# A two-block layer kernel on one core: the first layer's weight slabs in another order, one warming matmul less, and two small steps moved in the lead

## What is computed

```
xn = rms_norm(h, norm_mix[l])
proj = xn @ w_in[l]                       # 1024 x 7464
q, k, v, qi, ki, wi, sc_u, sc_b, sc_c, rw_z, gate_pre = split(proj)
q, k, qi, ki = partial_rope(...)          # rotation by position
y_a = dsa_attention(q, k, v, qi, ki, wi)  # top-64 by an index score
y_b = short_conv_mixer(...)
y_c = rwkv7_time_mix(rw_z, ...)
h = h + (sum over branches of sigmoid(gates) * (branch @ w_branch)) @ w_out
h = h + conv_glu_ffn(rms_norm(h, norm_ffn[l]), ...)
```

## Time and profile before

| | |
|---|---|
| Median of 3 runs | 1647.84 us (1647.72 to 1647.96) |
| The profiled execution | 1648.03 us, its span 1646.2 us |
| PE busy | 1632.2 us (99%), 11188 matmuls |
| DVE busy | 1188.4 us (72%) |
| ACT busy | 971.1 us (59%) |
| POOL busy | 187.3 us (11%) |
| Mean granted clock of PE | 0.999 |

### The profile page before, as it was taken

How to read it: one execution, slowest core, us unless ns; L and a number is a source line. 1 busy time by engine, 2 the same in 40 slices (tenths; PEclk the granted TensorE clock), 3 DMA queues, 4 the chain that set the end, 5 groups by cost and what they waited for, 6 DMA issues and landing times.

```text
span 1646.2 us, 27390 instructions
## 1 busy us (share of the span) xinstructions
PE 1632.2 (99%) x11188; PEld 1417.6 (86%) x11188; DVE 1188.4 (72%) x1666; ACT 971.1 (59%) x1485; POOL 187.3 (11%) x193
## 2 busy tenths in 40 slices
PE   9999999999999999999999999999999999999998
PEld 6999999988888999999988878778788887788886
DVE  7987447699888975547898885767756657667655
ACT  7674525555567565345555574665774556657743
POOL 0764400000002945100000000000000000000000
PEclk9999999999999999999999999999999999999999
DMA  7443534455545425525465546345445563444452
GB/s 277 169 154 115 188 104 135 173 186 197 186 170 202 161 97 162 166 90 191 138 225 190 189 164 217 128 135 176 141 167 178 181 209 133 146 163 152 141 192 77
DMA packets 48892, 270.11 MB, mean 164 GB/s; under 512 B 13632, under 2 KB 14656, under 8 KB 17024
## 3 DMA queue, kind: packets, MB, share of 16 engines
q1 hardware_dynamic: 38448, 265.22, 46.3%
q10 hardware_dynamic: 9712, 2.62, 0.7%
q0 software_dynamic: 608, 0.53, 0.2%
HBM read 266.51 MB, written 1.84 MB: 163 GB/s over the span
## 4 chain that ended last, share of the span: by engine, by line
PE 87%; DVE 9%; ACT 2%; issue 1%; DMA 1%; SPq 0%; DVEq 0%; ACTq 0%
PE bank L1768 15%; PE bank L1769 15%; PE bank L1773 15%; PE bank L1660 7%; PE bank L1705 7%; PE bank L1706 6%; PE bank L1710 6%; DVE w_low L1037 4%; PE bank L1665 3%; PE bank L2830 2%; DVE arena L1222 1%; PE bank L2130 1%; PE bank L2818 1%; PE bank L2862 1%; PE bank L2180 1%
## 5 line engine op out<-in xcount | busy, mean ns | idle before, releaser
L1037 DVE TENSOR_TENSOR w_low<-slab,w_high 128x2048 fp32r<-128x2048 f32 x249 | 574.1, 2314 | 203.5 <-ACT w_high L609 196.6
L609 ACT ACTIVATE w_high<-slab 128x2048 fp32r<-128x2048 f32 x249 | 470.5, 1896 | 110.0 <-PE bank L1773 89.3
L1768 PE MATMUL bank<-w_high,act 128*128 128x512 f32 x1120 | 444.4, 397 | 2.4 <-DVE arena L1231 1.0
L1769 PE MATMUL bank<-w_high,act 128*128 128x512 f32 x1120 | 437.1, 390 | 0.0
L1773 PE MATMUL bank<-w_low,act 128*128 128x512 f32 x1120 | 309.7, 390 | 0.0
L1705 PE MATMUL bank<-act,w_high 128*128 128x256 f32 x1024 | 258.6, 290 | 0.0
L1768 PEld LDWEIGHTS bank<-w_high,act 128*128 128x128 f32 x1120 | 210.4, 188 | 50.0 <-issue 6.9
L1706 PE MATMUL bank<-act,w_high 128*128 128x256 f32 x1024 | 251.7, 283 | 0.0
L1773 PEld LDWEIGHTS bank<-w_low,act 128*128 128x128 f32 x1120 | 210.2, 188 | 44.6
L1769 PEld LDWEIGHTS bank<-w_high,act 128*128 128x128 f32 x1120 | 210.6, 188 | 41.0
L1705 PEld LDWEIGHTS bank<-act,w_high 128*128 128x128 f32 x1024 | 195.8, 191 | 7.9 <-issue 5.6
(11 more groups left out here) (264 smaller groups left out, 1845.1 us busy)
## 6 DMA issues: line engine op xcount, KB each, us to landing
slab<-stream_a SPq DMA_DIRECT2D x143, 1024.0 KB, 4.9
slab<-stream_b SPq DMA_DIRECT2D x104, 1024.0 KB, 4.9
arena<-x_t SPq DMA_DIRECT2D x4, 256.0 KB, 6.9
slab<-stream_a ACTq DMA_DIRECT2D x2, 512.0 KB, 6.3
residual<-x_tok SPq DMA_DIRECT2D x1, 1024.0 KB, 11.6
lora_weights<-lora SPq DMA_DIRECT2D x2, 512.0 KB, 6.0
lora_weights<-final_rows SPq DMA_DIRECT2D x2, 512.0 KB, 6.1
d_inverse<-arena ACTq DMA_DIRECT2D x2, 256.0 KB, 4.0
```

Of the source, the lines that this page charges most:

```text
L609: line.did(eng.activation(core.wh[u % PARTS][:, 0:SLAB_WIDTH[u]], core.slab[u % SLABS][:, 0:SLAB_WIDTH[u]], ACT.Copy), core.sem("slab_high"))
L1037: line.did(line.eng.tensor_tensor(core.wl[u % PARTS][:, 0:SLAB_WIDTH[u]], core.slab[u % SLABS][:, 0:SLAB_WIDTH[u]], core.wh[u % PARTS][:, ...
L1768: eng.matmul(out, core.xh[:, at, columns_], wh[:, k, :], start=first and k == 0, stop=False, skip_group_check=True)
L1769: eng.matmul(out, core.xl[:, at, columns_], wh[:, k, :], start=False, stop=False, skip_group_check=True)
```

## The change

The first layer gets a list of units of its own in which ki stands second: w 0, ki, w 1, q 0, ... The plan's rows (products, banks) are kept and only change places. Because ki's products are counted late (at its turn, inside q 0), the part buffer of ki in a0 is given free by the count before it, three products (`row[2]`), which is the end of w 1. The host packs the first layer's stream in the new order. The lookups by position (`rows[u - 1]`, `UA["ki", 0]`, `first + u < 2`) are replaced by lookups by name. ki now waits for all of x. In the lead, the table load stands behind the rounding and split of slab 1 (now ki), and the rotation tables are copied there. The warming matmuls are five. The norm's spread and the steps behind it are put behind w 1, which is now the third unit. The list `behind_mid` stays as it was.

```
+UNITS_A0 = [UNITS_A[0], UNITS_A[2], UNITS_A[1]] + UNITS_A[3:]
...
+PLAN_A0 = [PLAN_A[0], PLAN_A[2], PLAN_A[1]] + PLAN_A[3:]
-PLANS = {"a0": PLAN_A, "a1": PLAN_A, "b0": PLAN_B, "b1": PLAN_B}
+PLANS = {"a0": PLAN_A0, "a1": PLAN_A, "b0": PLAN_B, "b1": PLAN_B}
...
-    SLAB_ENDS += [START[stage_].get("products", 0) + row[3] for row in PLANS[stage_]]
+    SLAB_ENDS += [START[stage_].get("products", 0) + (row[2] if stage_ == "a0" and row[0] == "ki" else row[3]) for row in PLANS[stage_]]
...
-        return steps + [("scaled", 2), ("scaled", 3), ("root_table", 0), ("round", 1), ("split", 1)]
+        return steps + [("scaled", 2), ("scaled", 3), ("round", 1), ("split", 1), ("root_table", 0), ("angles", 2)]
...
-        put(("w", 0), ("square", 0), ("square", 1), ("norm", 0), ("angles", 2))
+        put(("w", 0), ("square", 0), ("square", 1), ("norm", 0))
     amid(("w", 1), *([] if first else [("norm", 0)]), ("tables", 0))
-    put(("ki" if first else "w", 0 if first else 1), ("norm_x", 0))
-    put(("ki", 0), ("params", 0), ("highs", 0), ("lows", 0))
+    put(("w", 1), ("norm_x", 0))
+    put(("w", 1) if first else ("ki", 0), ("params", 0), ("highs", 0), ("lows", 0))
...
-    return woven(UNITS_A, first, lead_steps(first), after, mid, early=[("br2", 0), ("br2", 1)],
+    return woven(UNITS_A0 if first else UNITS_A, first, lead_steps(first), after, mid, early=[("br2", 0), ("br2", 1)],
                  late=[("br2", 1)], behind_mid=[("q", 0), ("gc", 2)] + [("w", 0)] * (not first))
...
+def unit_at(rows, kind, i):
+
+    return [row[0:2] for row in rows].index((kind, i))
...
+def first_fills(rows, u):
+
+    return rows[unit_at(rows, rows[u][0], 0)][4]
...
         if i and not begins:
-            eng.wait_ge(sem("slab_split").sem, 2)
+            eng.wait_ge(sem("slab_split").sem, u + 1)
...
     def ki(u):
 
         n, b = IDX_DIM + IDX_HEADS, rows[u][4][0][0]
+        eng.wait_ge(*sem("x_ready").upto(4))
         eng.wait_ge(sem("slab_split").sem, first + u + 1)
...
-    for _ in range(6):
+    for _ in range(5):
         eng.matmul(core.bank[6][:], flat(core, IDLE_)[:, 0:P], flat(core, IDLE_, 2), start=True, stop=True, skip_group_check=True)
...
-        for u, (kind, i) in enumerate(UNITS_A):
+        for u, (kind, i) in enumerate((UNITS_A0, UNITS_A)[layer]):
```

More of the change, by code:

```diff
@@ L706, in scalar_a @@
 def scalar_a(core, eng, line, stage):
-    rows, sem, bank, vec, layer = PLAN_A, core.sem, core.bank, core.vec, int(stage[1])
+    rows, sem, bank, vec, layer = PLANS[stage], core.sem, core.bank, core.vec, int(stage[1])
     def act(out, in_, func, tally=None, **kw):
@@ L795, in unit @@
                 made(core, eng, rows, u, m)
-                act(half_of(core, QS_ if kind == "q" else WS_, m), bank[rows[u - 1][4][m][0]][:], ACT.Copy, sem("qk_raw"),
+                act(half_of(core, QS_ if kind == "q" else WS_, m), bank[first_fills(rows, u)[m][0]][:], ACT.Copy, sem("qk_raw"),
                     scale=token_scale(core, m))
@@ L834, in ki_turn @@
     def ki_turn(_):
-        u = UA["ki", 0]
+        u = unit_at(rows, "ki", 0)
         b = rows[u][4][0][0]
@@ L1123, in vector_a @@
 def vector_a(core, eng, line, stage):
-    rows, sem, bank, vec, did = PLAN_A, core.sem, core.bank, core.vec, line.did
+    rows, sem, bank, vec, did = PLANS[stage], core.sem, core.bank, core.vec, line.did
     layer = int(stage[1])
@@ L1244, in unit @@
             for m in range(2):
-                b = rows[u - 1][4][m][0]
+                b = first_fills(rows, u)[m][0]
                 by = lambda ap, d: ap.rearrange("p (h d) -> p h d", d=d)
@@ L1297, in ki_turn @@
     def ki_turn(_):
-        b, spare = rows[UA["ki", 0]][4][0][0], flat(core, AROPE_, 2)
+        b, spare = rows[unit_at(rows, "ki", 0)][4][0][0], flat(core, AROPE_, 2)
         eng.wait_ge(*sem("qk_raw").next(eng, 2))
@@ L1824, in tensor_a @@
 def tensor_a(core, eng, banks, stage):
-    rows, sem, bank, first = PLAN_A, core.sem, core.bank, FIRST_SLAB[stage]
+    rows, sem, bank, first = PLANS[stage], core.sem, core.bank, FIRST_SLAB[stage]
     mm = eng.matmul
@@ L1872, in begin @@
             return
-        if first + u < 2:
+        if stage == "a0" and rows[u][0] == "w":
             first_units(u, True)
@@ L1879, in first_units @@
     def first_units(u, begins):
-        i, fills = u, rows[0][4]
+        i, fills = rows[u][1], rows[0][4]
         wh, wl = (w[u % PARTS][:].rearrange("p (k n) -> p k n", k=4) for w in (core.wh, core.wl))
@@ L1945, in ki_turn @@
     def ki_turn(_):
-        n, b = IDX_DIM + IDX_HEADS, rows[UA["ki", 0]][4][0][0]
+        n, b = IDX_DIM + IDX_HEADS, rows[unit_at(rows, "ki", 0)][4][0][0]
         eng.wait_ge(*sem("ki_copied").next(eng))
@@ L1957, in by_token_half @@
         wh, wl = (w[(first + u) % PARTS][:].rearrange("p (k n) -> p k n", k=4) for w in (core.wh, core.wl))
-        b = (fills if i == 0 else rows[u - 1][4])[m][0]
+        b = first_fills(rows, u)[m][0]
         if i == 0:
@@ L2272, in pool_a @@
 def pool_a(core, eng, line, stage):
-    rows, sem, did, vec, layer = PLAN_A, core.sem, line.did, core.vec, int(stage[1])
+    rows, sem, did, vec, layer = PLANS[stage], core.sem, line.did, core.vec, int(stage[1])
     tt = eng.tensor_tensor
```

2 lines of the change are left out of this document (1 added, 1 removed).

## The result

The changed kernel takes 1652.85 us in the median of 7 runs (1651.85 to 1653.6) against 1647.88 (1647.72 to 1648.1) before: a ratio of 1.0029, 95% interval 1.0020 to 1.0038. It is slower by 5.0 us; the forecast was 1652.6 in a range of 1650.0 to 1654.6. The profiled execution took 1652.29 us (span 1650.5), 4.3 over the one before.

A forecast was written before the change was run, and what follows sets the result against it. TensorE, busy 1632.2 of 1646.2 us, was taken as the bound, with q 0's start moving the end. Profiled 1648.03 + 3.48 (queue) + 1.9 (clock) - 0.6 (given back) = 1652.8, less 0.2 for the median: 1652.6, range 1650.0 to 1654.6.

The forecast's parts named there:

- The queue: Before q 0: rounding 4 and split 4 stand ahead of w 1's copies, tables and rotation; q 0 3.48 us later.
- The early gain: First three units, up to the spread's end: 1.4 us gained, not subtracted because it lies ahead of the wait.
- The clock: Wait before q 0: 5.9 us idle drops TensorE's clock to half rate, costing 1.9 us; chance of this case 0.66.
- rival 1: Wait before q 0 is there but the clock stays at 2.4 GHz: 1650.7 us; chance 0.23.
- Given back later: PE's wait for DVE at L2022 disappears because DVE is no longer late there: 0.6 us less.
- Faster: Rival: the 1.4 us of ki's move reach the end, q 0 starting by 23.6: 1646.4 us; chance 0.06.
- The delay: Rival: after the cold start DVE or ACT are late a second time, 1.9 us more: 1654.5 and over; chance 0.05.

The follow-up runs named there:

- e1: Changed kernel with rounding and split of slab 4 put behind unit w 1 instead of ahead of it; 1647.75 us, ratio 0.9999 to the kernel before.
- e3: Changed kernel with only DVE's split 4 put behind w 1, ACT's rounding 4 staying ahead of the copies; 1649.82 us, ratio 1.0012 to the kernel before.
- e11: Another profiled execution of the changed kernel with twenty products of q 0's slab and x, into an unread bank, in the wait for w 1's bank; 1650.52 us.
- e10: Profiled execution of the changed kernel with twenty products of q 0's slab and x, into an unread bank, in the wait for w 1's bank; 1653.53 us.
- e2: Changed kernel with six full-float matmuls on zeros behind the norm's spread, in the wait for w 1's bank; 1651.89 us, ratio 1.0030 to the kernel before.
- e7: Kernel before with five warming matmuls instead of six and nothing else; 1647.98 us, ratio 1.0000.
- e8: Changed kernel with rounding and split 4 behind w 1, tokens' transfer and first constants behind slab 3, squares, norm and tables behind ki; 1647.14 us.
- e9: Kernel before, ki still third and six warming matmuls, with tokens' transfer behind slab 3 and squares, norm and tables behind split 3; 1646.93 us, ratio 0.9994.

## Why the prediction was right

**The queue.** Rounding 4 ahead of the copies, split 4 ahead of tables and rotation, rounding 4 starting at 22.7: it started at 22.79, and q 0 at 28.60 where 28.5 was forecast. e1 is the proof: with these two steps behind w 1, and nothing else undone, the loss is gone. Of the two conditions of rounding 4 the forecast took the transfer (22.7) as the last; in the profile it was w 1's end, and the transfer had landed at 22.1. That both came out at the same figure was luck: w 1's end was forecast for 22.0, and was 22.7. The other profiles show either condition as the last: w 1's end in e3 (22.21) and e11 (22.43), the transfer in e10 (22.13) and e2 (23.70). From split 4's end to q 0 it took 28.60 - 27.02 = 1.58, as forecast.

**The early gain.** Here a term was mis-sized. w 0 was to start 0.4 earlier, at 7.6; it started at 8.37, since in this execution the passes of the warming matmuls stayed 0.85 apart until 7.46, where they were 0.43 apart from 5.41 on before (weight loads, first before, then after):

```profile
4.89 0.28 PEld L2261 LDWEIGHTS bank<-arena 128*128 128x128 f32 x1 [0.52 <-issue]
5.41 0.19 PEld L2261 LDWEIGHTS bank<-arena 128*128 128x128 f32 x1 [0.24 <-issue]
```

```profile
6.60 0.33 PEld L2274 LDWEIGHTS bank<-arena 128*128 128x128 f32 x1 [0.52 <-issue]
7.46 0.22 PEld L2274 LDWEIGHTS bank<-arena 128*128 128x128 f32 x1 [0.52 <-issue]
```

Ten passes took 7.62 us here and 5.97 in e7. The forecast treated one execution's step to the shorter spacing as fixed. So 0.9 of the 1.4 us was gained up to the spread's end (23.1 against 24.05). The prediction held that this gain does not count because it lies ahead of the wait; here part of it did, since w 1's end is also one of the conditions of rounding 4. With w 1 ended at 22.0, the transfer (22.1) would have been the last, and q 0 some 0.6 us earlier: an estimate from e3, where w 1 ended at 22.1 and rounding 4 started at 22.21 instead of 22.79. Two misses, w 1's end 0.7 later than forecast and the transfer 0.6 earlier, evened out.

**The clock.** That it would fall in the wait, given 0.66 + 0.05, was right; all seven runs of the changed kernel have a mean clock of 0.997 or 0.998 where the kernel before has 0.999 or 1.0. The cost, 1.9, is too high for the profiled execution: q 0's first half took 4.24 us against 27.95 - 25.02 = 2.93 before, so 1.31. The step that followed q 0's first half before:

```profile
27.95 0.31 PE L1950 MATMUL bank<-constants,arena 40*128 40x40 f32 x2
```

e11, where the clock held and the first half took 2.93 again (28.25 to 31.18), lies 1.77 under the changed kernel's profiled execution: 0.35 of that is q 0's start and 1.31 its first half. The 1.9 was read from the spacing of the warming passes, 0.85 against 0.43; that this is the clock was inferred, for the profile's granted clock reads 1.00 there:

```profile
1.00:5.10 4.10, 3.78 (x5) 1.72 (x6) 1.87 (x11) 1.49 (x2) 0.26 (x1) 1.00 0.70 185
```

In the changed kernel the clock was at 0.50 from 28.0 to 31.4, but q 0 began only at 28.60, so a part of the cold stretch fell into the wait and cost nothing. The forecast had all of it fall on work. Since the profiled execution lies 0.56 under the median, that the median (1652.85) came so close to 1652.6 is in part luck: what the other six runs spent on the clock was not profiled. The Trainium skill's rule (TensorE: Matmul & The Clock Gate, "HAM oscillation — how this bites in real kernels"), that a wait sends the clock back and the next work starts cold, is borne out by the 0.50 between 28 and 31 us. The fall of the clock decided between rival 1's 1650.7, where e11 is (1650.52), and the forecast.

**Given back later.** PE's 0.6 at L2022 is gone: 40.00 busy of 40.00 between 60 and 100 us, where it was 39.44 before:

```profile
60.00:100.00 40.00, 39.44 (x332) 37.55 (x331) 37.30 (x60) 20.52 (x33) 32.56 (x23) 1.00 0.48 162
```

Together 3.58 + 1.31 - 0.56 = 4.33, and the spans differ by 4.3.

**The rivals.** Faster (1646.4) needed split 4 ended by 23.44; it ended at 27.02. The delay did not spread: PE is busy for 27.00 of 27.00 us from 33 to 60. Two bounds of the forecast do not come out of its own terms: with rounding 4 from 22.0 on q 0 is 2.8 later, not 2.9, and the lower end of its own range is 1652.6 - 0.6 - 1.4 = 1650.6, not 1650.9; neither bears on the outcome. What remains open is the spread of the changed kernel's runs, 1.75 us against 0.38. How much of q 0's work falls into the cold stretch differs between profiles (2.8 us here, 3.4 in e3), and so does the spacing of the warming passes, which fits; but only one of the seven runs was profiled, so it is argued, not shown.

**Where the gain of ki's place went.** PE does finish the first three units earlier. In the changed kernel this ends in the longer wait; in e1, without the queue, in a wait of 2.42 for DVE's chain of split 3 and rotation; and e8 against e9 shows that with that chain shortened the old order is as good (1647.14 and 1646.93).

## What to carry to other kernels

When an order is woven by a rule such as "prepare the slab two ahead first", moving one unit changes which preparation stands ahead of every other unit's work; write out each engine's list for the new order and look for what now stands ahead of the step that frees a buffer. A gain that lies ahead of a wait is worth nothing until the wait's own chain is shorter: find the last instruction that ends the wait, and price the change there. A wait of several microseconds on TensorE can cost more than its length, since the clock can fall in it: 1.31 us here beside a wait of 5.47.

## What the runs showed that I had not expected

The clock can fall after the work has begun again: in e3 PE waited 3.24 us, resumed at 25.78, and the clock, still 1.00 up to 26, fell just before 27; in e10 PE waited 1.81 us, resumed at 673.73, and the clock fell at 675. The start is not fixed either: the same ten warming passes took 5.97 us in e7 and 7.62 in the changed kernel. And a transfer issued 4.3 us earlier (slab 4, 13.12 instead of 17.39) landed 0.6 earlier; the share of the transfer engines was 1.01 from its issue to its landing.
